# State-space stage in streamed chunks with all fronts first, and its cache copies in quarters beside the top-k

## What is computed

```python
    xbc_c = jax.nn.silu(causal_dwconv(conv_ext, conv_w, conv_b))
...
    dt = jax.nn.softplus(dt_raw.astype(jnp.float32) + dt_bias.astype(jnp.float32))
...
    acs = jnp.cumsum(dtc * A.reshape(G, HG), axis=2)
...
    decay = jnp.exp(jnp.where(causal[:, :, None, None], seg, -jnp.inf))
    cb = jnp.einsum('bcign,bcjgn->bcijg', Cc, Bc)
    y = jnp.einsum('bcijgh,bcjghp->bcighp', cb[..., None] * decay * dtc[:, :, None], xc)
...
    states = jnp.einsum('bclgn,bclghp->bcghpn', Bc, xc * to_end[..., None])
...
    def step(hc, inp):
        st, dec = inp
        return hc * dec[..., None, None] + st, hc
...
    y = y + jnp.einsum('bclgn,bcghpn->bclghp', Cc, h_in) * jnp.exp(acs)[..., None]
    y = y + xc * D.astype(jnp.float32).reshape(G, HG)[:, :, None]
...
    u = y.reshape(b, L, N_SSM_GROUPS, gs) * jax.nn.silu(z.astype(jnp.float32)).reshape(b, L, N_SSM_GROUPS, gs)
    u = u * lax.rsqrt(jnp.mean(u * u, axis=-1, keepdims=True) + RMS_EPS)
```

## Time and profile before

| | us |
|---|---|
| median of 3 runs | 2377.42 |
| lowest, highest | 2374.26, 2382.67 |
| the profiled execution, its own time | 2373.41 |
| its span, first to last instruction | 2371.6 |
| mean granted TensorE clock | 0.951 |
| PE busy | 2115.3 (89%) |
| DVE busy | 1569.7 (66%) |
| ACT busy | 745.9 (31%) |
| POOL busy | 803.7 (34%) |

### The profile page before, as it was taken

How to read it: one execution, slowest core, us unless ns; L and a number is a source line. 1 busy time by engine, 2 the same in 40 slices (tenths; PEclk the granted TensorE clock), 3 DMA queues, 4 the chain that set the end, 5 groups by cost and what they waited for, 6 DMA issues and landing times.

```text
span 2371.6 us, 34439 instructions
## 1 busy us (share of the span) xinstructions
PE 2115.3 (89%) x12253; PEld 1753.5 (74%) x12253; DVE 1569.7 (66%) x3260; ACT 745.9 (31%) x1111; POOL 803.7 (34%) x498
## 2 busy tenths in 40 slices
PE   7978998998678997999999989999888888898983
PEld 7978995555343347999999989999766666676762
DVE  1155215564443331169888979997888888898988
ACT  2122113443321002234444355554333232332321
POOL 2323320000110003346676621113544445565550
PEclk9999998999887998999999999999999999999996
DMA  9999987884996563225555578889999999999992
GB/s 351 348 357 347 350 326 292 328 353 180 324 323 230 176 240 99 71 95 171 173 171 171 170 243 293 295 287 366 388 394 394 394 394 380 395 395 394 392 393 76
DMA packets 200412, 682.81 MB, mean 288 GB/s; under 512 B 18432, under 2 KB 84352, under 8 KB 194304
## 3 DMA queue, kind: packets, MB, share of 16 engines
q1 hardware_dynamic: 151696, 508.36, 60.6%
q0 software_dynamic: 46080, 167.79, 18.5%
q10 hardware_dynamic: 2544, 5.48, 0.6%
HBM read 618.78 MB, written 196.32 MB: 344 GB/s over the span
## 4 chain that ended last, share of the span: by engine, by line
PE 35%; DMA 24%; issue 20%; DVE 14%; POOL 3%; ACT 3%; SPq 0%; ACTq 0%; DVEq 0%; POOLq 0%
DMA overlay<-peer_v 17%; PE bank L188 8%; PE bank L189 8%; PE bank L190 8%; DVE arena L1778 3%; DMA overlay<-peer_u 3%; DVE overlay L1955 3%; DMA overlay<-w_in 2%; PE bank L1765 2%; POOL overlay L341 2%; POOL overlay L1401 2%; DVE arena L1773 2%; PE bank L602 2%; PE bank L586 1%; PE bank L652 1%
## 5 line engine op out<-in xcount | busy, mean ns | idle before, releaser
L188 PE MATMUL bank<-overlay 128*128 128x384 f32 (+4 forms) x2856 | 989.0, 346 | 133.2 <-DVE overlay L1959 82.5
L189 PE MATMUL bank<-overlay 128*128 128x384 f32 (+4 forms) x2856 | 968.2, 339 | 0.0
L190 PE MATMUL bank<-overlay 128*128 128x384 f32 (+4 forms) x2856 | 966.4, 338 | 0.0
L188 PEld LDWEIGHTS bank<-overlay 128*128 128x128 f32 x2856 | 556.4, 195 | 199.3 <-issue 114.7
L190 PEld LDWEIGHTS bank<-overlay 128*128 128x128 f32 x2856 | 555.4, 194 | 33.5
L189 PEld LDWEIGHTS bank<-overlay 128*128 128x128 f32 x2856 | 556.9, 195 | 29.9
L1401 POOL TENSOR_TENSOR overlay<-overlay 128x1024 fp32r<-128x1024 f32 x98 | 262.6, 2682 | 207.2 <-ACT overlay L1393 207.1
L1610 POOL DMA_INDIRECT arena<-peer_rows,arena x160 | 182.6, 1141 | 366.3 <-DVE arena L1773 340.5
L1610 POOL DMA_INDIRECT arena<-peer_v,arena x160 | 228.7, 1429 | 172.0 <-DVE arena L1778 159.3
L1778 DVE SCALAR_TENSOR_TENSOR arena<-arena 128x1024 f32<-128x1024 f32 x160 | 203.9, 1275 | 0.4
L1773 DVE SCALAR_TENSOR_TENSOR arena<-arena 128x1024 f32<-128x1024 f32 x160 | 193.3, 1215 | 6.1 <-DMA arena<-peer_rows,arena 6.1
(11 more groups left out here) (221 smaller groups left out, 2028.8 us busy)
## 6 DMA issues: line engine op xcount, KB each, us to landing
overlay<-peer_u SPq DMA_DIRECT2D x128, 512.0 KB
overlay<-peer_v SPq DMA_DIRECT2D x128, 512.0 KB
o_ks<-cache_k SPq DMA_DIRECT2D x16, 4088.0 KB, 27.8
o_vsall<-cache_vall SPq DMA_DIRECT2D x16, 4088.0 KB, 40.1
arena<-cache_kT SPq DMA_DIRECT2D x32, 896.0 KB, 11.3
arena<-cache_v SPq DMA_DIRECT2D x56, 512.0 KB, 6.6
arena<-w_out SPq DMA_DIRECT2D x48, 512.0 KB, 4.8
act<-arena SPq DMA_DIRECT2D x128, 192.0 KB
```

The lines of the kernel that those rows point to most:

```text
L188: pe.matmul(out, lhs[0], rhs[0], start=start, stop=False)
L189: pe.matmul(out, lhs[0], rhs[1], start=False, stop=False)
L190: return pe.matmul(out, lhs[1], rhs[0], start=False, stop=stop)
```

## The change

**The SSD stage.** `xtok`, `btok`, `cbs` and the small exponentials now have a place for each chunk, `xdt`, `xw`, `yb` and the sums two places in turn. `xtok` takes the place of the stored v in `vz`, for which ACT now waits for 21 stores. The fronts of all five chunks (turning, sums, `cb`, their copies and small exponentials) come first, in banks 0 to 3 and 4 to 7 in turn. Then the chunks follow in one stream: `state` has moved from the end of a chunk to its start, `seg0` and `seg1` of the next chunk stand between `y2`, `y3` and what follows, and gate, squares, root and norm of chunk i - 1 stand within chunk i. `silu` works in place, and `xD` too. **The copies.** The ten copies of this stage are gone from there. Each is cut in four parts of 1022 KB (`copy_quarter`), and SP issues one part behind every second of the 80 key blocks. **The weights** of the output projection are issued each when its place is free, still behind the wait for the last `hn`.

```diff
-        eacs, wend, etot = small(456, H), small(472, H), small(488, H)
-        wsum = small(504, H)
+        eacs, wend, etot = small(0, TILES, H), small(348, TILES, H), small(456, QT, H)
...
+        def copy_quarter(sp, side, x, k):
+
+            src, dst = (("cache_k", "o_ks"), ("cache_vall", "o_vsall"))[side]
+            cutout = lambda ap, lo: ap.rearrange("b s d -> b (s d)")[:, bass.ds(x * CHUNK + lo, CHUNK)]\
+                .rearrange("b (s n) -> s b n", n=PIECE)[:, :, k * (PIECE // 4):(k + 1) * (PIECE // 4)]
             sp.dma_start(cutout(t[dst], 0), cutout(t[src], NT * D)).then_inc(copied, 16)
...
+        xtok = [cut(44 + 8 * i, D) for i in range(TILES)]
+        btok = [cut(118 + i, GR, N) for i in range(QT)] + [cut(18, GR, N)]
+        cbs = [cut(14 + i, GR, P) for i in range(QT)] + [cut(165, GR, P)]
+        xdt, xw = [cut(20, D), cut(187, D)], [cut(24, D), cut(191, D)]
...
+        yb, yu = [cut(36, D), cut(170, D)], cut(40, D)
...
-            for x in range(11, 16):
-                copy_cache(sp, 0, x)
-            for x in range(5):
-                copy_cache(sp, 1, x)
...
+            def front(i):
+                r, sfx, c0, b0 = rows(i), "" if i < QT else "_s", i * P, 4 * (i % 2)
+                if i == 1:
+                    pe.wait_ge(att_kept, H)
+                if i >= 2:
+                    act_ssd.wait(pe, i - 2, "cb_kept")
+                    dve_ssd.wait(pe, i - 2, "wdiff")
...
+            def seg(i, q):
+                r, sfx = rows(i), "" if i < QT else "_s"
+                pool_ssd.wait(pe, i, f"X{q}")
+                if 4 * i + q < 2:
+                    act_ssd.wait(pe, QT - 1, "x_kept")
+                else:
...
+            for i in range(TILES):
+                front(i)
+            seg(0, 0)
+            seg(0, 1)
+            for i in range(QT):
+                state(i)
+                intra(i, 0)
+                seg(i, 2)
+                inter(i)
+                intra(i, 1)
+                seg(i, 3)
+                intra(i, 2)
+                seg(i + 1, 0)
+                intra(i, 3)
+                seg(i + 1, 1)
+                if i:
+                    dve_ssd.wait(pe, i, "t_inter")
                     pe_ssd.count_done(i, "out_turned", turn_out(pe, i - 1, 0))
...
+            act.wait_ge(stored, 16 * SSD_STORES)
...
+            def silu_z(i):
+                z = vz[0:rows(i), i, D:2 * D]
+                act_ssd.count_done(i, "zsilu", act.activation(z, z, ACT.Silu))
...
+            decay(0, 0)
+            decay(0, 1)
+            for i in range(QT):
+                decay(i, 2)
...
+                    squares(i - 1)
+                decay(i, 3)
+                silu_z(i)
+                if i:
+                    root(i - 1)
+                decay(i + 1, 0)
+                decay(i + 1, 1)
...
+            differ(0)
+            differ(1)
+            inputs(0)
+            differ(2)
+            differ(3)
+            differ(4)
+            decayed(0)
+            masks(0, 0)
+            masks(0, 1)
+            for i in range(QT):
+                r = rows(i)
+                new_state(i)
+                if i:
+                    gated(i - 1)
+                masks(i, 2)
+                pe_ssd.wait(dve, i, "inter")
+                carried(i, 0)
+                masks(i, 3)
...
+                if i:
+                    normed(i - 1)
+                inputs(i + 1)
+                if i + 1 < QT:
+                    decayed(i + 1)
...
+                skip(i)
+                masks(i + 1, 0)
+                pe_ssd.wait(dve, i, "y3")
+                dve_ssd.wait(dve, i, "t_inter")
+                dve_ssd.count_done(i, "y_add", dve.tensor_tensor(by_head(yb[i % 2], r), by_head(yb[i % 2], r), two_banks(6, r), ALU.add))
+                masks(i + 1, 1)
+            gated(QT - 1)
+            masks(QT, 2)
+            masks(QT, 3)
+            normed(QT - 1)
+            skip(QT)
+            dve_ssd.wait(dve, QT, "xD")
+            pe_ssd.wait(dve, QT, "y3")
...
+            for i in range(3):
+                dve_ssd.wait(sp, i, "y_full")
+                weights(2 * i)
+                dve_ssd.wait(sp, i, "u")
+                weights(2 * i + 1)
+            pe_ssd.wait(sp, QT - 1, "inter")
+            dve_ssd.wait(sp, QT - 1, "hd")
+            weights(7)
+            pe_ssd.wait(sp, QT - 1, "state")
             pool_ssd.wait(sp, QT, "cmask1")
             sp.dma_start(lng, t["ln1_g"]).then_inc(ln_in, 16)
             sp.dma_start(lnb, t["ln1_b"]).then_inc(ln_in, 16)
+            dve_ssd.wait(sp, QT - 1, "y_full")
+            weights(6)
             residual(0)
...
-            with sp.Fori(0, EARLY // 4) as x:
-                for s in range(4):
-                    fetch(x * 4 + (s + 4), s, (u_lo, x * 4 + (s + QF + 1)))
-                    keep(x * 4 + s, s, x)
+            with sp.Fori(0, EARLY // 16) as x:
+                for k in range(4):
+                    for s in range(4):
+                        fetch(x * 16 + (4 * k + s + 4), s, (u_lo, x * 16 + (4 * k + s + QF + 1)))
+                        keep(x * 16 + (4 * k + s), s, x * 4 + k)
+                        if s % 2 == 1:
+                            copy_quarter(sp, k // 2, x + (11 if k < 2 else 0), k % 2 * 2 + s // 2)
...
-            sp.wait_ge(copied, 16 * 32)
+            sp.wait_ge(copied, 16 * (22 + 4 * 10))
```

426 lines of the change are left out of this document (222 added, 204 removed).

## The result

The changed kernel is **slower**: 2490.07 us (median of 4 runs, 2487.11 to 2493.64) beside 2378.19 (4 runs, 2374.26 to 2382.67) of the kernel before. The ratio is 1.0475, with a 95% interval of 1.0454 to 1.0495. The span of the profiled execution grew from 2371.6 to 2486.8 us, by 115.2. The forecast was 2338.1, a gain of 39.

The account below looks back on a forecast made before the run. The SSD stage was taken as bound by a chain through PE, ACT and DVE, no engine full. 2373.4 - 42.3 + 2 + 0 + 1 = 2334.1, a change of -39.3; from 2377.4 that gives 2338.1 us, range 2328 to 2346 (chance 0.68).

Parts of the forecast that it names:

- The SSD stage: Streaming the chunks, with a 22.4 us period, was to start the output projection at 690.3 instead of 732.57: -42.3 us.
- the clock: Low clock on PE in the SSD stage, behind gaps of 1 and 2.8 us a period: +2 us, between 0 and +11.
- Rival 1: SSD stream slower than its sum, as DVE meets POOL and PE's clock falls: 2346 to 2358 us, chance 0.19.
- Rival 2: Each ACT table change in the SSD stage costs a 1.3 us drain: 7.8 us more, 2345.9 us, chance 0.04.
- The output projection: Behind the SSD stage, it keeps its order and length: 0, between -2 and +2 us.
- The copies: Quarter copies beside the key blocks: the DMA queue keeps up, +1 us, between 0 and 3.2.
- The slack: In the key blocks, a fetch landing 3.2 us later leaves 4.8 of 8.0 us of slack; ACT's wait fits too.
- The size of a quarter: A quarter copy beside the key blocks takes 3.2 us, so copies and loads need 7.8 of 8.45 us.
- Rival 3: Copies starve the key blocks: a 5.5 us quarter costs 66 us, 2404 us, slower than before; chance 0.03.
- Its sign: In the key blocks, PE waiting for POOL's split of the keys would show copies starving them; no size given.
- The rest of the +1: After the key blocks, the last quarter and three fetches meet small transfers before the gathers: +1 us, between 0 and 3.2.
- The queue rule: DMA engines take a ring's descriptors in order, so a key-block fetch behind a quarter copy lands 3.2 us later.

Follow-up runs that it names:

- copies_moved_alone: The kernel before, with only its ten cache copies moved, in quarters, beside the key blocks; 2529.33 us, ratio 1.0663 to the kernel before.
- no_copies: The changed kernel with the ten cache copies left out altogether; 2338.63 us, ratio 0.9857 to the kernel before.
- fetch_early: The changed kernel with each key-block fetch issued one block earlier, ahead of the keep and quarter copy; 2398.85 us, ratio 1.0096 to the kernel before.
- early_pair_runs: The changed kernel with fetches issued a block earlier and quarters cut as two sequences in 32.7 KB runs; 2340.90 us, ratio 0.9846 to the kernel before.
- pair_runs: The changed kernel with each quarter cut as two whole-piece sequences, 32 runs of 32.7 KB, same place and queue; 2382.19 us, ratio 1.0014 to the kernel before.
- seven_and_three: The changed kernel without quarters: seven whole copies in the SSD stage, three behind output projection weight tiles; 2356.85 us, ratio 0.9919 to the kernel before.

## Why the prediction was wrong, point by point

- **The SSD stage was right.** The forecast for the time from E3 of chunk 0 to the output projection was 17.9 + 22.4 + 22.4 + 18.9 = 81.6 us, plus 2 for the clock; it took 18.8 + 22.3 + 23.9 + 18.8 = 83.8. E3 of chunk 0 came at 613.3 instead of 608.7, since DVE started 4.4 us later than in the earlier trace rows: the attention ahead ended 3.2 us later (first record of the stage 583.36, before 580.18), and `ssm_norm_g` came 5.1 us after its issue, before 3.9. The 3.2 us are scatter between profiled runs and not the stream's doing: copies_moved_alone, whose attention and SSD stage are those of the kernel before, issues `ssm_norm_g` 4.1 us later than that kernel (585.08 and 580.95). Counted from the stage's own first record, the stream took off 38.6 us (152.4 to 113.8) of the 42.3 forecast. The output projection started at 697.2, against 690.3 + 2. Rival 1 did not come. PE waited 1.2 to 2.0 us per period for L1263, where 2.8 was worked out, and from the second period on 1.61 us more for L1174 ahead of `state`, the gap of 1 us that the paragraph on the clock names: 3.6 us in all, beside 3.8. The 1.7 us by which the third period was longer are the clock: `y0` and the first product of `seg2` took 1.59 and 2.02 us there (667.11 and 668.48), 1.10 and 1.08 a period before (644.84 and 645.78).
- **Rival 2 (a drain with each table load) did not come**: silu starts 0.01 us behind the end of its load (613.36 + 1.28, 614.65).
- **The output projection** was right (161.5 us before, 161.7 after). It was right also that nothing behind gives the stream's gain back: no_copies keeps all of it (35.7 us).
- **The copies were wrong, in two steps.** The forecast was +1; they cost 151.
  - *The slack.* The prediction put the later fetch against 8.0 us of slack up to PE, as a single delay in a chain with an end. It is a loop: the fetch is issued after a gelu, which comes after an in-order `hi_of`, which waits for a fetch. The sentence that ACT's wait "fits as well" compared one wait with one gelu, and did not go round. Round two blocks, with the prediction's own quarter of 3.2 us, the sum would have been 2.14 (keep, quarter and fetch issued, a price that only the changed trace shows) + 3.8 (a fetch issued at 1354.61 released ACT at 1358.44) + 3.2 + 0.95 = 10.1 us, more than the 8.45 it had in hand: 40 x 1.65 = 66 us lost, and a forecast of about 2404. Without the quarter the sum is at most 2.14 + 3.8 + 0.95 = 6.9 us, under 8.45: in the kernel before the loop exists too and does not hold, and PE is full. Its waits gave only a faint sign, the 0.58 us of ACT for the fetch in the earlier trace rows: ACT waited so 45 times between the 11th and the 71st keep, 17.1 us in all and never over 1.6.
  - *The size of a quarter.* 3.2 us came from whole copies, with runs of 32.7 KB. The change's quarter has runs of 8.2 KB and asks for 4.9 us of the engines (by the lowest product 4.4). 4.6 + 4.9 = 9.5 is over 8.45 even without the loop., which I held against it, had loads of 4 KB runs but whole copies, so no short copy was in it. fetch_early, where the loop is open, shows what this step costs alone: 2398.9 us, 60 above the run without copies. The sum gives 40 x 1.1 = 44 of them, so some of it stays open.
  - In the changed kernel both meet: with the quarter of 4.9 us, and keeps and fetches queued behind it, the landing grew to 9.3 us, and the loop to 12.4. 79 blocks at 6.01 instead of 4.20 us are the 142.7 us of the table.
- **Rival 3 had one of the two bounds, with less than half of the price.** It put copies that starve the key blocks at 2404 for a quarter of 5.5 us, by the engines' rate alone. The quarter came to 4.9, for which its own sum gives 42 us and a kernel as fast as before. The loop's other 91 us were in none of the rivals. Its sign came (PE waited 77.6 us for POOL's split, L1535), but that sign can't tell the rate from the loop.
- **The rest of the +1**, for the last quarter and three fetches ahead of the gathers, was sound in itself: with both bounds mended (early_pair_runs) the stretch behind the 80th keep is 0.7 us longer than without copies. In the changed kernel it is 7.7 us longer than before, for a reason that isn't shown.
- **The queue rule** (a fetch waits behind the copy ahead of it) is borne out in part. Taking the copies to another queue removed 60 of the 151 us, perhaps in part by the issue that left SP's queue; with the copy on another queue the fetch still lands after 7.8 us, beside 3.6 without copies.

## What to carry to other kernels

A transfer that is put "beside" a stage must be laid against every closed loop through its queue, not against the slack of the next reader: add issue, landing and every in-order step round the loop, and divide by the blocks the loop spans. Prefetching one block deeper breaks such a loop without a byte less. Price a copy by its own runs: here the same megabyte was worth 2.4 to 4.9 us of the DMA engines, by how it was cut.

## What the runs showed of the hardware that I had not expected

- The cut of a DRAM-to-DRAM copy of 1022 KB over 16 engines: 32 runs of 32.7 KB (two sequences) took 2.4 to 2.5 us of the DMA engines by share times period, 128 runs of 8.2 KB 4.1 to 4.9, with two sequences and with eight. With the engines full, a pair of blocks took 9.76 us with the short runs from eight sequences and 8.73 with those from two.
- With an outermost size of 4 instead of 16 the same bytes made a pair take 16.6 us at a DMA share of 0.43, though share times period stayed at 7.1 us, as in pair_runs.
- PE waited for its loads at a DMA share of only 0.77: the idle time of the DMA engines lay in a latency loop, and the pair became shorter (9.76 us at 0.98) as soon as the loop was opened.
- In seven_and_three a single wait of 4.0 us was followed by a mean clock of 0.66 over the window from 750 to 770 us, and the projection took 172.6 us instead of 161.7: the clock cost 6.2 us, more than the wait.
